# Last layer's experts: picking seven of the eight token pairs by row fetches and transposes in place of PE products

## The reference, cut to what matters

```python
def moe(h, w_router, b_router, w_e_gate, w_e_up, w_e_down):
    aff = sigmoid(h @ w_router); sel = aff + b_router
    ...                                   # best of 4 groups, then its top 2 experts, by sel
    gates = w_top / sum(w_top) at top_idx, else 0
    for e in range(16):
        he = silu(h @ w_e_gate[e]) * (h @ w_e_up[e])      # 1024 -> 512
        y = y + gates[:, e:e+1] * (he @ w_e_down[e])      # 512 -> 1024
```

## Time and profile before

| what | value |
|---|---|
| three timed runs | 1530.07, 1532.04, 1532.34 us; median 1532.04 |
| profiled execution | 1531.17 us, span 1529.3 us |
| mean granted clock of TensorE | 0.951 of full speed |
| busy share of the span: PE, DVE, ACT, POOL | 91%, 52%, 44%, 11% |
| data moved by DMA | 357.96 MB, mean 234 GB/s |

### The profile page before, as it was taken

The page is one execution under the profiler, slowest core; times in us unless marked ns, Lnnn a source line. Parts: engine busy times, 40 slices in busy tenths (PEclk is TensorE's granted clock), DMA queues, the critical chain, the costliest instruction groups (busy, mean ns, idle before and its releaser), DMA issues.

```text
span 1529.3 us, 21505 instructions
## 1 busy us (share of the span) xinstructions
PE 1395.5 (91%) x8088; PEld 1049.5 (69%) x8088; DVE 800.0 (52%) x1312; ACT 670.1 (44%) x1104; POOL 166.9 (11%) x188
## 2 busy tenths in 40 slices
PE   5699999999998995899999992999998897999995
PEld 2378777886556873778888872998885695655641
DVE  1512335424774626799999974567427665111113
ACT  3532223224665315578888864563246633000001
POOL 4210110001330000041111102000000000000001
PEclk9699999999998997799999996999999898999998
DMA  8674565334882232699999984355332158999996
GB/s 294 230 276 150 193 206 192 91 94 154 261 258 82 84 124 90 202 383 390 397 377 376 368 320 172 107 147 174 107 114 69 56 166 335 415 415 415 415 415 248
DMA packets 116054, 357.96 MB, mean 234 GB/s; under 512 B 13889, under 2 KB 14210, under 8 KB 115330
## 3 DMA queue, kind: packets, MB, share of 16 engines
q1 hardware_dynamic: 91410, 272.86, 48.6%
q0 software_dynamic: 23984, 81.85, 15.1%
q10 hardware_dynamic: 576, 2.10, 0.3%
HBM read 341.38 MB, written 25.69 MB: 240 GB/s over the span
## 4 chain that ended last, share of the span: by engine, by line
PE 83%; DMA 7%; DVE 5%; ACT 3%; issue 2%; POOL 0%; SPq 0%; POOLq 0%; DVEq 0%; ACTq 0%
PE ps L578 19%; PE ps L580 18%; PE ps L579 18%; PE ps L1194 6%; PE ps L1216 3%; PE ps L844 3%; PE ps L977 2%; PE ps L1000 2%; PE ps L1177 2%; DMA w_raw<-in_w_ada 1%; DMA ring<-in_w_e_down 1%; DMA ring<-in_w_e_up 1%; PE ps L988 1%; PE ps L1134 1%; DMA ring_h<-in_w_e_down 1%
## 5 line engine op out<-in xcount | busy, mean ns | idle before, releaser
L574 DVE TENSOR_TENSOR w_lo<-w_raw,w_hi 128x1024 fp32r<-128x1024 f32 x224 | 270.1, 1223 | 309.5 <-ACT w_hi L570 307.9
L570 ACT ACTIVATE w_hi<-w_raw 128x1024 fp32r<-128x1024 f32 x224 | 235.5, 1058 | 321.4 <-PE ps L580 317.6
L578 PE MATMUL ps<-h_hi,w_hi 128*128 128x512 f32 (+1 forms) x704 | 249.3, 354 | 11.1 <-issue 5.7
L580 PE MATMUL ps<-h_hi,w_lo 128*128 128x512 f32 (+1 forms) x704 | 247.3, 351 | 0.0
L579 PE MATMUL ps<-h_lo,w_hi 128*128 128x512 f32 (+1 forms) x704 | 247.1, 351 | 0.0
L578 PEld LDWEIGHTS ps<-h_hi,w_hi 128*128 128x128 f32 x704 | 134.2, 191 | 33.7 <-issue 9.6
L580 PEld LDWEIGHTS ps<-h_hi,w_lo 128*128 128x128 f32 x704 | 134.1, 190 | 18.7
L579 PEld LDWEIGHTS ps<-h_lo,w_hi 128*128 128x128 f32 x704 | 134.3, 191 | 18.2
L574 DVE TENSOR_TENSOR w_lo_more<-w_raw,w_hi_more 128x1024 fp32r<-128x1024 f32 x96 | 114.9, 1222 | 4.5
L570 ACT ACTIVATE w_hi_more<-w_raw 128x1024 fp32r<-128x1024 f32 x96 | 101.2, 1060 | 21.7 <-PE ps L580 19.3
L549 POOL DMA_DIRECT2D w_raw<-in_w_ada x96 | 68.8, 724 | 356.7 <-PE ps L844 350.1
(11 more groups left out here) (303 smaller groups left out, 2510.7 us busy)
## 6 DMA issues: line engine op xcount, KB each, us to landing
w_raw<-in_w_ada POOLq DMA_DIRECT2D x96, 512.0 KB, 5.5
w_raw<-in_w_e_gate SPq DMA_DIRECT2D x64, 512.0 KB
w_raw<-in_w_e_up SPq DMA_DIRECT2D x64, 512.0 KB
w_raw<-in_w_e_down SPq DMA_DIRECT2D x64, 512.0 KB
w_raw<-in_w_in SPq DMA_DIRECT2D x56, 512.0 KB
ring<-in_w_e_up SPq DMA_DIRECT2D x40, 512.0 KB, 13.7
ring<-in_w_e_gate SPq DMA_DIRECT2D x38, 512.0 KB
w_raw<-in_w_gate SPq DMA_DIRECT2D x32, 512.0 KB
```

What stands on the lines that cost most here:

```text
L570: act.activation(whi(n), raw[:, slot(n), :, :], ACT.Copy).then_inc(hi_ready, 1)
L574: dve.tensor_tensor(wlo(n), raw[:, slot(n), :, :], whi(n).bitcast(F32), ALU.subtract).then_inc(lo_ready, 1)
L578: pe.matmul(acc, sh, mh, start=first, stop=False, skip_group_check=True)
L580: return pe.matmul(acc, sl, mh, start=False, stop=last, skip_group_check=True)
```

## The change

Pair 0 is still picked by PE products (now `pick_pair`). For pairs 1 to 7 the last layer does what the first does:

- ACT writes the two tiles of `h2rows` to `hbuf` (`act.dma_start` now in both layers; `h_out` and `y_free` become one semaphore per layer).
- PE finds the token numbers of pairs 1 to 7 with 14 tiny products (`pair_ids`), after the first gate product; DVE turns them into `ids`, between `tokens_b(0)` and `places(i)`, which therefore comes later.
- POOL fetches the rows of a pair from `hbuf` into `xg` (two buffers) with an indirect DMA: pairs 1 and 2 at once, pair p+3 after the store of expert 2p. Slots without a token have a number past the end, and are skipped.
- `turn_pair(p)` waits for the fetch and transposes 8 blocks instead of multiplying 16 pairs of blocks.
- `h2rows` moves to the last 8 KB of rG, and `xg` takes its old place. So the ring's slots move: slots 24 to 27 are now in rH, and wait for the last copy into `h2rows` (before: 26 to 29); slots 28 and 29 lie where `h2rows` is, and wait for `pick_pair` and for the writes to `hbuf`.
- `pick1` gets the type float32r; `last_rows(0)` waits for `ids_out`, since both use bank 7; the slow path reads `hbuf` in both layers.

```diff
-    h2rows = view("h2_rows", [P, 2, D], F32, rQ)
+    h2rows = view("h2_rows", [P, 2, D], F32, rG + 24 * KB)
-    pick1 = view("pick1", [P, 4, NE, HC], F32, rG)
+    pick1 = view("pick1", [P, 4, NE, HC], F32R, rG)
...
-        if k < 26:
+        if k < 24:
             return ring_g[:, k - 20 if k < 22 else k - 18, :, :]
-        return ring_h[:, k - 26, :, :]
+        return ring_h[:, k - 24, :, :] if k < 28 else ring_g[:, k - 22, :, :]
...
-                    elif n == RING - 4:
+                    elif n == RING - 6:
                         wait_emptied(sp, (i, "h2", 3, 1))
+                    elif n == RING - 2:
+                        sp.wait_ge(u_t, NE + 1)
+                        sp.wait_ge(h_out[i], 16 * len(tiles[i]))
...
+                def fetch(p):
+                    if p >= 3:
+                        pool.wait_ge(u_t, NE + p - 1)
+                    pool.indirect_dma_start(xg[:, p % 2, :], None, hbuf, bass.IndirectOffsetOnAxis(ap=ids[:, p:p + 1], axis=0),
+                                            bounds_check=T - 1, oob_is_err=False).then_inc(u_in[p % 2], 16)
...
+                pool.wait_ge(h_out[i], 16 * len(tiles[i]))
+                pool.wait_ge(ids_out, 4)
+                fetch(1)
+                fetch(2)
                 pool.wait_ge(rt_loc[i], 1)
                 pool.wait_ge(pad_out, 16 * (ROWS // P))
                 for e in range(HELD):
                     store(e)
+                    if e % 2 == 0 and e // 2 + 3 < NE // 2:
+                        fetch(e // 2 + 3)
...
+            def pair_ids():
+
+                pe.wait_ge(picked, 8)
+                for p in range(1, NE // 2):
+                    for t in tl:
+                        m = pe.matmul(ps[:, 7, 2 * p:2 * p + 2], pick1[:, t, 2 * p:2 * p + 2, :], tokr[:, t, :],
+                                      start=t == tl[0], stop=t == tl[-1], skip_group_check=True)
+                m.then_inc(ids_done, 1)
...
             def turn_pair(p):
-                pe.wait_ge(picked, 4 + p // 2 + 1)
-                if p:
-                    pe.wait_ge(u_xa, NE + p)
-                    pe.wait_ge(u_xb, NE + p)
+                pe.wait_ge(u_in[p % 2], 8 * NE + 16 * ((p + 1) // 2))
+                pe.wait_ge(u_xa, NE + p)
+                pe.wait_ge(u_xb, NE + p)
+                for k in range(KT):
+                    d0 = (k // CK) * CK * P + k % CK
+                    m = pe.transpose(ps[:, 5 + k // 4, (k % 4) * P:(k % 4 + 1) * P], xg[:, p % 2, d0:d0 + CK * P - 1:CK], ident)
+                m.then_inc(u_t, 1)
+
+            def pick_pair():
+
+                pe.wait_ge(picked, 5)
                 for k in range(KT):
                     d0 = (k // CK) * CK * P + k % CK
                     for t in tl:
                         m = pe.matmul(ps[:, 5 + k // 4, (k % 4) * P:(k % 4 + 1) * P], h2rows[:, t - 2, d0:d0 + CK * P - 1:CK],
-                                      pick1[:, t, 2 * p:2 * p + 2, :], start=t == tl[0], stop=t == tl[-1],
+                                      pick1[:, t, 0:2, :].bitcast(F32), start=t == tl[0], stop=t == tl[-1],
                                       skip_group_check=True)
                 m.then_inc(u_t, 1)
...
                 if k == 0:
+                    pe.wait_ge(ids_out, 4)
...
-                turn_pair(0)
+                pick_pair()
                 for e in range(NE):
                     into_hidden1("g", e)
+                    if e == 0:
+                        pair_ids()
...
-                    if half and i == 0:
+                    if half:
                         wait_emptied(act, key)
-                        act.dma_start(hbuf[t * P:(t + 1) * P, :], rows).then_inc(h_out, 16)
+                        act.dma_start(hbuf[t * P:(t + 1) * P, :], rows).then_inc(h_out[i], 16)
...
                 tokens_b(0)
+                dve.wait_ge(ids_done, 4)
+                dve.tensor_scalar(ids[:, 1:NE // 2], ps[:, 7, 2:NE:2], float(FAR), None, ALU.add).then_inc(ids_out, 1)
                 places(i)
```

More of the change, by code:

```diff
@@ L352, in build @@
         "o_ss", "o_std", "o_nrm", "ot_h", "ot_l", "m_f", "m_h", "m_l")
-    rt_asg, rt_loc, f_sort = per_layer("rt_asg", "rt_loc", "f_sort")
-    h_out, y_free = sem("h_out"), sem("y_free")
+    rt_asg, rt_loc, h_out, y_free, f_sort = per_layer("rt_asg", "rt_loc", "h_out", "y_free", "f_sort")
     e_out = [[sem(f"e_out_{i}_{j}") for j in range(2)] for i in range(DEPTH)]
@@ L361, in build @@
         sem(f"e_{k}") for k in ("xt", "xh", "xl", "sig", "he", "ht", "hh", "hl", "ya", "yd"))
-    u_t, u_xa, u_xb, u_sg, u_he, u_ht, u_hc, u_y = e_xt, e_xh, e_xl, e_sig, e_he, e_ht, e_hl, e_ya
+    u_in, u_t, u_xa, u_xb, u_sg, u_he, u_ht, u_hc, u_y = e_in, e_xt, e_xh, e_xl, e_sig, e_he, e_ht, e_hl, e_ya
     f_go, f_in, f_dn, f_out, f_pe, f_act, f_dve = per_layer("f_go", "f_in", "f_dn", "f_out", "f_pe", "f_act", "f_dve")
@@ L726, in _ @@
             if i == 0:
-                pool.sem_inc(y_free, 2)
+                pool.sem_inc(y_free[i], 2)
                 def fetch(e):
@@ L740, in store @@
                         pool.wait_ge(e_out[i][(e - 1) % 2], 16 * ((e + 1) // 2))
-                        pool.sem_inc(y_free, 1)
+                        pool.sem_inc(y_free[i], 1)
                     pool.indirect_dma_start(ybuf, bass.IndirectOffsetOnAxis(ap=row_of[0:cap, e:e + 1], axis=0),
@@ L744, in store @@
                                             bounds_check=ROWS - 1, oob_is_err=False).then_inc(e_out[i][e % 2], 16)
-                pool.wait_ge(h_out, 16 * len(tiles[i]))
+                pool.wait_ge(h_out[i], 16 * len(tiles[i]))
                 wait_emptied(pool, (i, "ids", 0))
@@ L783, in _ @@
                     pool.wait_ge(pad_out, 16 * (ROWS // P))
+                for t in tiles[i]:
+                    pool.dma_start(y1[:, t, :], hbuf[t * P:(t + 1) * P, :]).then_inc(f_sort[i], 16)
+                pool.wait_ge(f_sort[i], 16 * len(tiles[i]))
+                for s in range(2):
                     for t in tiles[i]:
[L785 to L798, removed]
+                        pool.indirect_dma_start(hsort, bass.IndirectOffsetOnAxis(ap=loc[:, s, t:t + 1], axis=0),
+                                                y1[:, t, :], None).then_inc(f_sort[i], 16)
+                pool.wait_ge(f_sort[i], 48 * len(tiles[i]))
                 pool.sem_inc(f_go[i], 1)
@@ L1595, in result @@
                 act.wait_ge(w_used, scaled(n, it, 24))
-                act.wait_ge(y_free, e + 1)
+                act.wait_ge(y_free[i], e + 1)
                 act.activation(ytile[0:cap, j, 0:CW], ps[0:cap, 2, :], ACT.Copy).then_inc(e_ya, 1)
@@ L1613, in _ @@
                 splits(nb, 4)
-                act.wait_ge(h_out, 16 * len(tiles[i]))
+                act.wait_ge(h_out[i], 16 * len(tiles[i]))
                 tokens_hi(0)
@@ L1990, in places @@
                 for t in range(2):
-                    dve.tensor_tensor(weighed[:, t, :, :, :], spread(pick1[:, 2 + t, HELD:, :].unsqueeze(2), [P, 2, 2, HC]),
+                    dve.tensor_tensor(weighed[:, t, :, :, :], spread(pick1[:, 2 + t, HELD:, :].bitcast(F32).unsqueeze(2), [P, 2, 2, HC]),
                                       spread(ta[:, 2 + t, HELD:].unsqueeze(2).unsqueeze(3), [P, 2, 2, HC]), ALU.mult)
@@ L2092, in result @@
                 dve.wait_ge(w_used, scaled(n, it, 24))
-                dve.wait_ge(y_free, e + 1)
+                dve.wait_ge(y_free[i], e + 1)
                 dve.tensor_copy(ytile[0:cap, j, CW:D], ps[0:cap, 3, :]).then_inc(e_yd, 1)
```

## The result

The changed kernel takes 1538.03 us (median of 9 runs), the kernel before 1529.42 (9 runs, among them the three shown ahead). The ratio is 1.0055, 95% interval 1.0038 to 1.0073: 8.4 us slower by the ratio (5.8 to 11.2), 8.6 by the two medians. The profiled execution took 1540.59 us, its span is 1538.8.

What follows compares the result with a forecast made beforehand. The full weight stream, not PE, was taken as the last stage's bound. Writes 2.5, fetches 4.6 and skew 0.4 gave 7.5 us more, so 1539.5 us; own range 1536.5 to 1542.5, 8 in 10 within 1534 to 1546.

Steps and rivals of the forecast that it cites:

- The bound: Last stage: the weight stream at 415 GB/s sets the end; PE's time doesn't count while its ring ends dry.
- Turns: PE, pairs 1 to 7: 1.22 us for 3.97 each, 19.3 us less in all, 0 us off the end.
- waits some 18 + 7 us more: Sign of being right: PE runs dry near 1375, not 1453, and waits that much more for ring chunks.
- Bytes: Added to the weight stream: 1.05 MB of writes, 2.5 us, and 1.85 MB of fetches, taken as 4.6 us.
- Writes: Two tiles to hbuf at about 1279 and 1280: 1.05 MB, 2.5 us, not hidden; landing within a few us.
- Skew: Fetches' empty slots load DMA engines unevenly: 0.4 us added; upper bound for the fetches 9.2 us.
- Sum: End of the kernel: 2.5 + 4.6 + 0.4 = 7.5 us more; last ring chunk lands 6 to 9 us later.
- Gates, fetch waits, `places`: Later ring slots, fetches before turns, places behind ids: no stream gap, 0 us; at worst 1 us of PE, hidden.
- A: Rival, chance 0.06: PE is the bound up to 1452, so the change is faster, about 1517 to 1525.
- B: Rival, chance 0.13: fetches load half the engines (+4.6 us more) or a gate opens late (up to 6): 1544 to 1550.
- C: Rival, chance 0.04: the clock drops; if for all of 1370 to 1508, PE becomes the bound, 1560 or more.
- D: Rival, chance 0.09: nothing moves, the added bytes find room in the stream, 1531 to 1534.5.

Runs made afterwards that it cites:

- e1: Changed kernel without its added transfers (no writes to hbuf, no fetches; transposes read stale rows): ratio to the kernel before 1.0007, 1.1 us.
- e4: Kernel before with the change's bytes alone (ACT writes h2rows, POOL copies seven times 64 rows memory to memory): ratio 1.0064, 9.8 us slower.
- e8: Changed kernel with every turn of pairs 1 to 7 done three times: ratio to the kernel before 1.0051, 7.8 us slower.
- e7: Kernel before with the products of pairs 1 to 4 done twice: ratio 1.0023, 3.5 us slower.
- e3: Changed kernel without the two writes to hbuf, fetches kept: ratio to the kernel before 1.0059, 9.0 us slower.
- e2: Changed kernel with the two writes to hbuf but without the fetches: ratio to the kernel before 1.0038, 5.8 us slower.
- e6: Changed kernel with four ring slots of rG filled early (chunks 8 to 11): ratio to the kernel before 1.0030, 4.6 us slower.
- e5: Kernel before with six ring slots in rG filled early (chunks 8 to 13): ratio 0.9972, 4.3 us faster.

## Why the prediction was right, point by point

- *The bound.* Right. The DMA share stayed at 1.03 and 415 GB/s after 1290, as named ahead; e1, e4 and e8 show it, and e7 its limit: PE becomes the bound when it gets more than 12 us of work. The chain's 83% for PE fell to 78%, with no gain.
- *Turns.* 1.16 us each against a predicted 1.22, `pair_ids` 1.65 against 1.6. The ring ran dry at 1380 (predicted near 1375). Off the end came 0 us, as said. The sign "waits some 18 + 7 us more" is right, but PE's idle time alone doesn't show it. Counted as in e7, idle time rises by 13.1 us (8.4 to 21.5), while the same gate and up products count as busy for 8.6 us more (128.0) and the down products for 3.5 more (64.7): 25.2 us in all.
- *Bytes.* 2.98 MB against 2.90: the seven fetches were 1.93 MB, not 1.85. The step "experts 0 and 1 then hold about 61" was the guess in it: 1.93 MB is 471 rows, so pair 0 holds about 41. At 415 GB/s 7.2 us against 7.1.
- *Writes.* The term was a little too small. Not the count of bytes but the rate while they are in flight: 337 GB/s in the changed kernel, so 4 x (1 - 337 / 420) = 0.8 us more. They landed 8.8 us after their issue (median of the two), not "within a few us"; slot 28 was still opened by the end of `pick_pair`.
- *Skew.* Wrong in kind, small in size. The 0.4 us were put on the fetches' empty slots; e1 and e3 show the uneven end with and without fetches. The last 8 us of stream leave 4 x (1.03 - 0.88 + 1.03 - 0.33) = 3.4 us of engine time unused after the change, 3.6 in e1, 2.9 before (0.94 and 0.40 by the same count). The half microsecond more belongs to the spread, so that the 0.4 us were about the right size is luck.
- *Sum.* 7.2 + 0.8 + 0.5 = 8.5 us against 8.8 in the stream and 8.4 in the time. The forecast had 7.5: it lacked the 0.8. As a place in the trace, the last chunk is read 9.7 us later (1514.11 to 1523.78), outside the named 6 to 9; 0.9 us of that is the later issue of chunk 8.
- *Gates, fetch waits, `places`.* No cost: e1 has gates, and no gap (+0.8 us, of which the tail is 0.7). POOL issued the first fetch at 1298.91, PE turned pair 1 at 1310.24, right behind the up product; predicted 1309.
- *Rivals.* A is refuted by e1 (1528.3 against the 1514 it asked for) and e8. B: no stretch is under full between 1290 and 1508. C: the granted clock was 1.00 from 1300 to 1508 while PE was 82% to 91% busy in the stretches from 1380 on with transposes in them, so the rule of the Trainium skill on transposes ("TensorE: Matmul & The Clock Gate", PE-mode transpose) had no effect here; in e8, with three times the transposes, it was 1.00 as well. In the last 6 us of the stream, where PE had been waiting for the last chunks (busy for 1.08 of the 2 us from 1516), it did fall, to 0.79 and 0.50; in the kernel before it fell only behind 1514, to 0.65 and 0.50. That cost nothing to speak of: from the read of the last chunk to the end of the span it is 15.0 us, 15.2 before. (In e6 it was 0.98 and 0.97 in the stretches 1340 to 1440 and 1440 to 1500; no reason shows, and the stream was full.) D is refuted by e2 and e4. The rule of the Trainium skill on DMA engines 7 and 15 ("DMA: Bandwidth & Descriptors", latency and other measured facts) can't be tested, since the trace doesn't split engines; that fetches lengthen the end is not seen.
- *The median.* The prediction stood on 1532.0 for the kernel before; over nine runs it is 1529.4, so a cost of 8.6 us led to 1538.0 and not to 1540.6. The baseline was 2.6 us too high and the cost 1.1 us too low; that the two misses mostly cancel is luck.

What stays open: in time e2 and e3 lie 3 to 4 us over what their streams show, e5 lies 1.6 under. The streams add up (2.6 + 5.2 = 7.8 of 8.8 us), the times don't (5.8 + 9.0 = 14.8 against 8.4). For e2 and e3 the stream's figure lies outside the interval of the time, so the spread of the runs alone doesn't explain it. The mixer's end, which the change doesn't touch, moves by 7 us between these executions (and in e5's it was later still), and the kernel before itself has medians of 1529.42, 1527.29 and 1528.49 us in its three sets of runs. No run says what moves them; I don't claim more than the streams for e2 and e3.

## What to carry to other kernels

When two engines look full, ask which has a reserve: a ring of 30 chunks let PE look like the bound for 160 us while the stream of weights set the end. Then every byte counts, and an instruction counts only when PE's reserve (12 us in the kernel before) is used up, and a change that trades 18 us of PE work for 3 MB of traffic loses 8 us. The reserve is best measured by adding work that changes nothing else, since busy time counts a part of the waiting. What helps such a stage is to start the stream earlier, up to the point where the ring is full before its first reader comes.

## What the hardware showed that I had not expected

Writes of 4 KB rows beside a full stream of reads lower the rate that the busy engines move: 337 to 350 GB/s over 4 us in five kernels (after, e2, e4, e6, e8: share 0.96 to 1.01), against 419 to 420 in the same stretch of those without writes (before, e1, e3). Why isn't shown. Alone, in the first layer, such writes went at 424 GB/s. The fetches, which are reads, show no such dip: the stretch from 1300 to 1320 of the changed kernel, with three of POOL's transfers in it, runs at a share of 1.03 and 413 GB/s. POOL's stores are writes too, but of some 30 rows each: by the same ratio a store would cost 0.1 us, which these stretches can't show. And a write of 512 KB that lands in 3.0 us alone took 8.2 to 8.8 us beside the stream (medians of the five kernels).
